# One layer of a hybrid encoder on one core: differential heads in pairs, contiguous transposes in the experts, w_ada's second part read one group earlier

## What is computed

```
mod = c @ w_ada + b_ada                       # sh1, sc1, g1, sh2, sc2, g2, 1024 each
h   = rms(x) * (1 + sc1) + sh1
p   = h @ w_in                                # 8192 columns
oa  = differential attention, 8 heads: (softmax(q1 k1') - lam * softmax(q2 k2')) @ v   # head size 64, v 128
ob  = stick-breaking attention, 16 heads of size 64
x   = x + g1 * ((sigmoid(ga) * (rms(oa) @ w_pa) + sigmoid(gb) * (ob @ w_pb)) @ w_o)
h   = rms(x) * (1 + sc2) + sh2
top 4 of 32 experts for each row (router_w), softmax gates
expert: g, u = split(h @ w_gu + b_gu); (clip(u) + 1) * min(g, 7) * sigmoid(1.702 min(g, 7)) @ w_down + b_down
x   = x + g2 * sum over the chosen experts;  out = rms(x) * final_g
```

## Time and profile before

| | us |
|---|---|
| median of 3 runs | 1372.65 (1372.52 to 1375.13) |
| profiled execution, its own time | 1371.69 |
| its span, first to last instruction | 1369.7 |
| TensorE busy | 1298.5 (95%) |
| VectorE busy | 468.8 (34%) |
| ScalarE busy | 186.5 (14%) |
| memory, mean over the span | 349 GB/s, 477.55 MB |
| mean granted TensorE clock | 0.992 |

### The profile page before, as it was taken

One profiled execution on the slowest core, in us unless ns is written; L12 is line 12 of the kernel. 1 busy time (PEld: TensorE's weight loads), 2 busy tenths in 40 slices (PEclk: granted clock), 3 DMA queues, 4 the chain that ended last, 5 costly groups with the idle time before them and its releaser, 6 DMA issues.

```text
span 1369.7 us, 16175 instructions
## 1 busy us (share of the span) xinstructions
PE 1298.5 (95%) x5988; PEld 608.3 (44%) x5989; DVE 468.8 (34%) x924; ACT 186.5 (14%) x378; POOL 15.6 (1%) x48
## 2 busy tenths in 40 slices
PE   4999999999999999999999999999999986999996
PEld 2876876778853333333333333333333332333332
DVE  1020766333134332333334342343423332324333
ACT  2101322333011000100001000010001000001001
POOL 0000000110000000000000000000000000000000
PEclk9999999999999999999999999999999999999999
DMA  9746758224668999999999999999999999399993
GB/s 364 255 160 246 246 185 298 103 91 171 263 266 349 406 431 429 429 429 428 428 428 429 428 428 429 388 421 429 428 429 429 429 429 428 151 428 429 428 428 155
DMA packets 55983, 477.55 MB, mean 349 GB/s; under 512 B 4863, under 2 KB 4948, under 8 KB 28308
## 3 DMA queue, kind: packets, MB, share of 16 engines
q1 hardware_dynamic: 55652, 476.11, 84.5%
q10 hardware_dynamic: 304, 1.06, 0.2%
HBM read 476.10 MB, written 1.05 MB: 348 GB/s over the span
## 4 chain that ended last, share of the span: by engine, by line
PE 89%; DMA 7%; ACT 1%; DVE 1%; issue 1%; SPq 0%; DVEq 0%
PE bank L1500 31%; PE bank L1533 16%; PE bank L1204 13%; DMA down_ring<-in_w_down 5%; PE bank L1452 4%; PE bank L1489 4%; PE bank L1322 4%; PE bank L1195 4%; PE bank L1467 3%; PE bank L1385 2%; DMA gu_ring<-in_w_in 2%; PE bank L1461 2%; ACT scratch L657 1%; PE bank L1478 1%; PE bank L1283 1%
## 5 line engine op out<-in xcount | busy, mean ns | idle before, releaser
L1500 PE MATMUL bank<-gu_ring,scratch 128*64 128x512 f32 x2048 | 462.1, 598 | 5.8 <-issue 4.2
L1500 PEld LDWEIGHTS bank<-gu_ring,scratch 128*64 128x64 f32 x2048 | 143.5, 137 | 289.7 <-issue 285.8
L1533 PE MATMUL bank<-down_ring,scratch 128*64 128x512 f32 x1024 | 227.3, 596 | 1.9 <-DMA down_ring<-in_w_down 1.9
L1204 PE MATMUL bank<-gu_ring 128*128 128x256 f32 x768 | 174.3, 385 | 2.2 <-DMA gu_ring<-in_w_in 2.2
L1204 PEld LDWEIGHTS bank<-gu_ring 128*128 128x128 f32 x768 | 146.1, 193 | 25.4 <-issue 4.7
L1533 PEld LDWEIGHTS bank<-down_ring,scratch 128*64 128x64 f32 x1024 | 70.4, 137 | 134.5 <-issue 126.2
L1024 DVE TENSOR_TENSOR scratch<-bank,bgu 128x512 f32<-128x512 f32 x32 | 22.1, 692 | 280.5 <-PE bank L1467 280.5
L661 ACT ACTIVATE scratch<-bank 128x512 f32<-128x512 f32 x32 | 19.1, 597 | 708.7 <-PE bank L1500 708.7
L1006 DVE TENSOR_TENSOR xres<-xres,bank 128x512 f32<-128x512 f32 x132 | 81.9, 682 | 38.7 <-PE bank L1489 38.7
L1038 DVE TENSOR_TENSOR scratch<-bank,scratch 128x512 f32<-128x512 f32 x32 | 22.1, 692 | 182.0 <-PE bank L1533 182.0
L1452 PE MATMUL bank<-xn,onehot 128*64 128x512 f32 x264 | 71.2, 618 | 0.0
(11 more groups left out here) (258 smaller groups left out, 775.4 us busy)
## 6 DMA issues: line engine op xcount, KB each, us to landing
gu_ring<-in_w_gu SPq DMA_DIRECT2D x128, 2048.0 KB, 21.3
down_ring<-in_w_down SPq DMA_DIRECT2D x64, 2048.0 KB, 14.4
gu_ring<-in_w_in SPq DMA_DIRECT2D x32, 1024.0 KB, 7.9
gu_ring<-in_w_ada SPq DMA_DIRECT2D x20, 1024.0 KB, 7.0
down_ring<-in_w_ada SPq DMA_DIRECT2D x4, 1024.0 KB, 10.3
gu_ring<-in_w_pa SPq DMA_DIRECT2D x4, 1024.0 KB, 6.2
gu_ring<-in_w_pb SPq DMA_DIRECT2D x4, 1024.0 KB, 6.6
gu_ring<-in_w_o SPq DMA_DIRECT2D x4, 1024.0 KB, 10.3
```

What stands on the lines that cost most here:

```text
L1204: last = M(dst[:, b * T:(b + 1) * T], group_chunk(group, kt // 4)[:, kt % 4, cols], hT[:, kt, :], start=kt == 0, stop=kt == KT - 1)
L1500: last = M(bank[f // 2][64 * a:64 * a + 64, :], xT[:, kt % 4, kt // 4, :], gu_ring[:, 8 * half + kt, f * 512:(f + 1) * 512], start=kt == 0 ...
L1533: last = M(bank[7][64 * a:64 * a + 64, :], act_sb[:, kt % 4, kt // 4, :], down_ring[:, kt // 2, (kt % 2) * D + a * 512:(kt % 2) * D + (a + ...
```

## The change

The differential step handles one map of two heads in place of two maps of one head, and VectorE combines two heads in each even step; transposition and value product come one step later (12 steps in place of 11). The w_ada groups stand one place earlier in the load order and are read one place earlier by VectorE; the partition sum and the columns of the second part come two projection halves earlier. In an expert, the gate parts of kt 5, 6 and 7 are given before the up parts; the transposes of the gate values stand between up parts 5 and 6. ScalarE's copies write contiguous blocks and read the bank with steps instead. The way back comes after the taking, VectorE makes the activation in two halves, down begins after the first half, and the transposes of the taken rows stand in the middle of down. Dummy products (`keep_busy`) are added in the first part of w_ada.

```diff
-GROUPS = ([("in", g) for g in range(4)]
-          + [(w, g) for g in range(4, 12) for w in ("in", "ada")] + [("in", g) for g in range(12, 16)]
+GROUPS = ([("in", g) for g in range(3)]
+          + [group for g in range(3, 11) for group in (("in", g), ("ada", g + 1))] + [("in", g) for g in range(11, 16)]
...
             def differential(s):    # ScalarE
-                    for m in range(2):
+                    m = s % 2
+                    for i in range(2):
...
-                if s >= 2:
-                    h = s - 2
+                if s >= 3:
+                    h = s - 3
...
-                    if (g, h) == (8, 0):
+                    if (g, h) == (7, 0):
                         copy_rows(1)
...
-                A(x_raw, bank[4][:, :], ACT.Copy).then_inc(xraw_ready, 1)
+                A(x_raw.rearrange("s (b r p) -> s b r p", b=2, r=2), by_pairs(bank[4][:, :]), ACT.Copy).then_inc(xraw_ready, 1)
...
-                A(g_raw, bank[0][:, :], ACT.Copy).then_inc(raw_ready, 1)
+                A(in_blocks(g_raw), by_fours(bank[0][:, :]), ACT.Copy).then_inc(raw_ready, 1)
                 act.wait_ge(gu_used, item * 8 + 8)
-                A(u_raw, bank[1][:, :], ACT.Copy).then_inc(raw_ready, 1)
+                A(in_blocks(u_raw), by_fours(bank[1][:, :]), ACT.Copy).then_inc(raw_ready, 1)
...
-                copy_back(item)
                 copy_taken(item + 1)
+                copy_back(item)
...
-            ada_products(4)                  # VectorE
-            ada_products(5)
+            for g in range(4, 7):
+                ada_products(g)
...
+            for s in range(DAH + 4):
+                if s % 2 == 0 and 2 <= s <= DAH:
+                    for i in range(2):
+                        dve.wait_ge(exp_ready, 4 * s + 2 * i - 2)
+                        combine(s - 2 + i)
...
-                if s % 2 == 1 or s == DAH + 2:
-                    ada_products(6 + s // 2)
+                if s % 2 == 1 and s < DAH + 2:
+                    ada_products(7 + s // 2)
...
-                own.then(V.tensor_tensor(u_sb, blocks(3), wide(bias[:, 8:16]), ALU.add))
-                own.then(V.tensor_scalar(u_sb, u_sb, LIMIT, -LIMIT, ALU.min, ALU.max))
-                V.scalar_tensor_tensor(act_sb, u_sb, 1.0, sig, op0=ALU.add, op1=ALU.mult).then_inc(act_ready, 1)
+                for a in range(2):
+                    u, u_bias = u_sb[:, :, a, :], bias[:, 8 + 4 * a:12 + 4 * a].unsqueeze(2).to_broadcast([P, 4, CAP])
+                    own.then(V.tensor_tensor(u, blocks(3)[:, :, a, :], u_bias, ALU.add))
+                    own.then(V.tensor_scalar(u, u, LIMIT, -LIMIT, ALU.min, ALU.max))
+                    V.scalar_tensor_tensor(act_sb[:, :, a, :], u, 1.0, sig[:, :, a, :], op0=ALU.add, op1=ALU.mult
+                                           ).then_inc(act_ready, 1)
...
+                if kt in (4, 5, 6):          # TensorE, first part of w_ada
+                    keep_busy(3, 6)
             last.then_inc(ada_first, 1)
+            keep_busy(2, 6)
             ada_columns(0)
+            keep_busy(7, 6)
...
-                    for m in range(2):       # TensorE, differential(s)
-                        q = qkT[part, 0, 4 * m + blk, :]
-                        k = qkT[part, 0, 8 + 4 * m + blk, :]
-                        dst = bank[2 + m]
-                        M(dst[:, 0:128], q[:, 0:P], k[:, 0:P], start=True, stop=True)
-                        M(dst[:, 128:384], q[:, P:T], k, start=True, stop=True).then_inc(scores_done, 1)
+                    for n in range(2):
+                        for i in range(2):
+                            part = slice(64 * i, 64 * i + 64)
+                            q, k = qkT[part, 0, 4 * m + blk, :], qkT[part, 0, 8 + 4 * m + blk, :]
+                            if n == 0:
+                                M(bank[2 + i][:, 0:128], q[:, 0:P], k[:, 0:P], start=True, stop=True)
+                            else:
+                                M(bank[2 + i][:, 128:384], q[:, P:T], k, start=True, stop=True).then_inc(scores_done, 1)
...
-                    if kt < KT - 2:          # TensorE, expert
+                    if kt < KT - 3:
...
+                gate_up(KT - 3, (2, 3))
+                pe.wait_ge(raw_ready, item * 2 + 1)
+                transposes(2, g_raw).then_inc(gT_done, 1)
                 gate_up(KT - 2, (2, 3))
-                pe.wait_ge(raw_ready, item * 2 + 1)
-                transposes_by_fours(2, g_raw).then_inc(gT_done, 1)
                 gate_up(KT - 1, (2, 3))
                 pe.wait_ge(given_added, item * 4 + 4)
-                way_back(item)
                 take(item + 1, (0,))
                 pe.wait_ge(raw_ready, item * 2 + 2)
-                transposes_by_fours(3, u_raw).then_inc(uT_done, 1)
+                transposes(3, u_raw).then_inc(uT_done, 1)
                 take(item + 1, (1,))
-                take_transposed(item + 1)
-                pe.wait_ge(act_ready, item + 1)
+                way_back(item)
                 for kt in range(KT):
+                    if kt == KT // 2:
+                        take_transposed(item + 1)
+                    if kt % (KT // 2) == 0:
+                        pe.wait_ge(act_ready, item * 2 + (1 + 2 * kt // KT))
```

More of the change, by code:

```diff
@@ L1117, in _, with keep_busy @@
             M = nc.tensor.matmul
+            def keep_busy(count, b):
+                for _ in range(count):
+                    M(bank[b][:, 0:P], ident[:], ones[:], start=True, stop=True, skip_group_check=True)
             pe.wait_ge(consts, 2)
@@ L1412, in rank @@
                 M(bank[2 + tt][:, 0:NE], before[:], sel[:, tt, :], start=not tt, stop=True).then_inc(rank_done, 1)
-            def keep_busy(count, b):
-                for _ in range(count):
-                    M(bank[b][:, 0:P], ident[:], ones[:], start=True, stop=True, skip_group_check=True)
             take_turn(TURN_G2B + 2)
@@ L1455, in take, with transposes @@
                     last.then_inc(taken_done, 1)
-            def transposes_by_pairs(b, src):
+            def transposes(b, src):
                 for j in range(4):
-                    first = (j // 2) * 2 * P + j % 2
-                    last = nc.tensor.transpose(bank[b][:, j * P:(j + 1) * P], src[:, first:first + 2 * P - 1:2], ident[:])
-                return last
-            def transposes_by_fours(b, src):
-                for j in range(4):
-                    last = nc.tensor.transpose(bank[b][:, j * P:(j + 1) * P], src[:, j:4 * P:4], ident[:])
+                    last = nc.tensor.transpose(bank[b][:, j * P:(j + 1) * P], src[:, j * P:(j + 1) * P], ident[:])
                 return last
@@ L1568, in further @@
                 pe.wait_ge(f_raw, k + 1)
-                transposes_by_fours(2, g_raw).then_inc(f_guT_done, 1)
+                transposes(2, g_raw).then_inc(f_guT_done, 1)
                 pe.wait_ge(y_ready, expert + 1)
```

106 lines of the change are left out of this document (55 added, 51 removed).

## The result

| us | before | after |
|---|---|---|
| median | 1373.46 (1372.52 to 1375.13, 5 runs) | 1366.64 (1364.33 to 1368.88, 5 runs) |
| ratio, 95% interval | | 0.995 (0.994 to 0.9961) |
| profiled execution, its own time | 1371.69 | 1364.33 |
| its span | 1369.7 | 1362.4 |

The change makes the kernel 0.5% faster. The forecast was 1359.0 us with a range up to 1366: its sum was 12.7 us, and in the profiled executions 7.4 came (6.8 between the medians).

What follows compares the result with a forecast made beforehand. Loads were taken to bound the middle of the expert stage, TensorE the time before 444.53 and the last seven experts. Gains of 7.4 and 5.3 us, together 12.7, off 1371.69 gave 1359.0 us, range 1355.5 to 1366.

Steps and rivals of the forecast that it cites:

- Pairs, 5.2 us: Score products of two heads run together, 0.85 us a step instead of 1.50; eight times 0.65 gives 5.2 us.
- The covers that were named for VectorE's later steps and for the group order: Ahead of the experts: waits and early reads hide VectorE's later steps (cost nothing) and the group order (0 to 1 us, taken 0).
- Start clock, 0.8 of bounds 0 and 2.8: As the projection begins, dummy products may end the half clock: 0 to 2.8 us gained, 0.8 taken.
- Their own cost is nothing: At the start, the 18 dummy products fall into TensorE's waits, so they were taken to cost no time.
- The rule: From item 1's first down load (444.53) to the landing at 1147.7, loads at 4.89 us each set time; faster TensorE gains nothing.
- the 1.25 us of item 0: Item 0's first half of down comes 1.25 us sooner: 0.75, and 0.5 of transposes now behind it.
- Last seven, 7 x 0.75: Experts 25 to 31, after 1147.7, never wait for loads; each gains about 0.75 us, together 5.3.
- the 0.127 each: Expert transposes from contiguous columns cost 0.127 us each against 0.17 strided; three groups of four save 0.54 us.
- VectorE's chain: In an expert, VectorE's gated product and up values hold back down: about 0.5 us of wait comes back.
- Slower copies: Rivals on ScalarE's copies in an expert: 1.5 times as long, 1363.8 us, chance 0.12; twice as long, 1375.5, chance 0.06.
- Pairs not concurrent: Rival: banks or VectorE's order keep the heads' score products from running together; 5.2 us missing, 1364.2, chance 0.05.
- Clock lost in the further pass: Rival: in expert 25's further pass, longer load waits drop TensorE's clock to half near 1138; 1364.5 us, chance 0.22.

Runs made afterwards that it cites:

- e13: The kernel before with the pairs of heads, moved group order and earlier partition sum alone, no dummy products: 1368.38 us, ratio to before 0.9967.
- e4: The kernel after without the 18 dummy products at the start: 1369.59 us, ratio to before 0.9988.
- e8: The kernel after with 14 one-column dummy products in an idle stretch near 10 us: 1362.92 us in one execution, before 1369.81.
- e9: The kernel after with 8 one-column dummy products in the idle stretch near 10 us: 1363.24 us, ratio to before 0.9925.
- e14: The kernel before with 8 one-column dummy products in the idle stretch near 10 us: 1377.3 us, ratio to before 1.0038.
- a1: The kernel after, unchanged, timed again: 1366.7 us, ratio to before 0.9952.
- e5: The kernel after with ScalarE's sigmoid of the gate values ahead of its copy of the up values: 1363.46 us in one execution, before 1369.81.
- e6: The kernel after with the taken rows' transposes ahead of down again, not between its halves: 1363.48 us in one execution, before 1369.81.
- e10: e9 with dummy products in the further pass of odd experts: 1359.74 us, ratio to before 0.9907.
- e11: e9 with ScalarE's sigmoid ahead of its copy of the up values: 1357.86 us, ratio to before 0.9891.
- e1: The kernel before with the expert-stage part of the change alone: 1372.78 us, ratio to before 1.0001.
- e12: e9 with both the dummy products in the further pass and the sigmoid ahead of the up copy: 1357.36 us, ratio to before 0.9883.

## Why the prediction was wrong

Its direction and its mechanism held; the size did not. Point by point:

- **Pairs, 5.2 us**: 5.33 (e13). Right. The covers that were named for VectorE's later steps and for the group order held: the last transposes came 7.94 us sooner with nothing lost on the way.
- **Start clock, 0.8 of bounds 0 and 2.8**: 2.6 in after's profiled execution. I took the value near no gain because the added work was small; it removed nearly all of the half clock (full from 35 us on). The rule of the Trainium skill (TensorE: Matmul & The Clock Gate, Part 1) quoted in the prediction was the better guide here. 1.8 us too little.
- **"Their own cost is nothing"** (the 18 dummy products), and with it the whole passage between the heads and item 0: this is the step that failed. Their time was nothing, but their place in the code moved the block border, and that cost 2.6 us of idle time and 1.5 us of half clock at the entry. Shown by e4 (without them the entry is short), e8, e9 and e14; e4 shows as well that without them a stall of 2.68 us stands in item 1 instead. No term and no rival of the prediction had it, though before's profile shows 0.42 us of "issue" inside item 1, with a transfer of queue 8 that starts 2.5 us ahead of the product behind it.
- **The rule**: "between the first down load of item 1 and the landing at 1147.7 time is loads" was right in kind, since 3.85 us at the loop's first issue became 4.45 at 865.59. Its start was put 21 us late: the 1.25 us of item 0 counted in full, and in after's profiled execution 0.6 of them came. By a1, e8 and e9, which have the same item 0 and 446.87 to 447.10 us from first issue to landing against before's 446.80, even those are chance.
- **Last seven, 7 x 0.75**: 0.35 each. Two terms of the sum were mis-sized: a transposition of four was 0.09 cheaper and not 0.18 (the 0.127 each came from three transposes in another place), and VectorE's chain kept TensorE 0.61 us and not 0.5. e5 and e6 show that 0.45 more was to be had from either end.
- **Rivals.** Slower copies are out: 0.60 us. What the prediction took for them from the Trainium skill (Advanced Engine Details and Errata, Memory Cachelines) is said there of products, and the step from products to ScalarE's copies was its own. Pairs not concurrent: out. *Clock lost in the further pass* did come in part: it fell at 1123.79, and the pass ran with three stretches of half clock. e9, e10 and e11 put the price at 2.2 to 4.5 us, by how long the clock happens to be down. In after's own sum it hardly shows, because before lost some clock behind the pass too.

Against the forecast of 12.7: start clock +1.8, entry -4.1, item 0 -0.6, last seven -2.8 (7 x 0.40); 7.0 is left, and 7.4 was measured. The difference of 0.4 lies between 865.59 and the last seven (order switch and pass) and is not taken apart. That this sum comes out so near is partly luck: a second profiled execution of the same kernel (a1) was 0.4 us sooner at the entry, had 1.3 us more of half clock there and 0.9 more in the load chain.

## What to carry to other kernels

A loop that jumps over a long block of code has a price that depends on how many instructions stand ahead of it: after any change upstream, look at the idle time marked "issue" behind each jump, and at the queue that carries instructions. Dummy products or a few added lines can cost there more than they bring. "Issue" alone does not prove a fetch: 3.73 us of it stand before expert 25 in before (1158.28) and 3.78 in after, and queue 8 brings nothing between 452.9 and 1354.6 us in before; what those are is open. It takes the transfer, and a run in which the code is moved. And where an operation is moved to fill a gap, ask whether the other moves have already closed that gap; its switch then costs without return.

## What was not expected of the hardware

- A block of instructions is a transfer of 16 KB, and 2.6 us pass from its start to the next product (411.58 to 414.23 in after, 421.6 to 424.20 in e14). The stall in item 1, behind its first product, was 0.42 us in before, 0.25 in e13, 2.68 in e4 and 4.58 in e1. Its length goes with the start of the transfer: the next product comes 2.2 to 2.6 us behind it in all four (446.2 to 448.77 in before, 441.0 to 443.27 in e13, 443.9 to 446.11 in e4, 450.0 to 452.20 in e1), and it starts 1.5 us ahead of item 1's first product in before and 3 us behind it in e1. What sets off the transfer was not tried and stays open.
- The granted clock after the same 1.6 us of idle time was full in eight profiled executions (before, e1, e4, e8, e10, e11, e12, e13) and half for 3.4 us in a ninth (e9). After 2.07 us it was full in e10, after 2.03 at the same place in e12 it fell.
- Transposes with a contiguous source load their weights in 141 ns instead of 209, but four of them gain only 0.09 us.
